# An attention stage reordered on TensorE, with small moves on ScalarE and VectorE around it

## The reference

```
h = rms_norm(x, norm_mix_pre)
z, xbc, dt_raw, q, k, v = jnp.split(h @ w_in, split_at, axis=-1)
s = jnp.einsum('bhcqd,bhckd->bhcqk', qb, k) * scale
s = jnp.where(causal, s, -jnp.inf)
p = jax.nn.softmax(s, axis=-1)
attn = p[:, :, 0] - lam * p[:, :, 1]
o = jnp.einsum('bhqk,bhkv->bhqv', attn, v)
k_mem = (mem_h @ wk)
```

## Time and profile before

| | us |
|---|---|
| median of 3 runs (lowest, highest) | 1418.82 (1418.66, 1419.02) |
| the profiled execution | 1418.83 |
| its span, first to last instruction | 1417.1 |
| TensorE busy | 1399.2 |
| VectorE busy | 943.2 |
| ScalarE busy | 666.8 |

### The profile page before, as it was taken

How to read it: one execution, slowest core, us unless ns; L and a number is a source line. 1 busy time by engine, 2 the same in 40 slices (tenths; PEclk the granted TensorE clock), 3 DMA queues, 4 the chain that set the end, 5 groups by cost and what they waited for, 6 DMA issues and landing times.

```text
span 1417.1 us, 19418 instructions
## 1 busy us (share of the span) xinstructions
PE 1399.2 (99%) x7146; PEld 1172.0 (83%) x7146; DVE 943.2 (67%) x1516; ACT 666.8 (47%) x1297; POOL 70.6 (5%) x122
## 2 busy tenths in 40 slices
PE   9999999999989999999999999999999999999997
PEld 7889888876779888888888888888888888888886
DVE  4785577748878336344555888886665685467897
ACT  6225332347776325333433765454444654444443
POOL 0000000010002002010001200000000000000011
PEclk9999999999999999999999999999999999999999
DMA  9212333320014522121133235654443897676463
GB/s 328 67 43 67 91 97 97 97 72 18 1 31 149 208 75 105 60 74 46 60 119 109 100 97 201 218 198 156 164 156 117 297 356 247 225 236 196 153 229 128
DMA packets 98909, 194.45 MB, mean 137 GB/s; under 512 B 11200, under 2 KB 29696, under 8 KB 96768
## 3 DMA queue, kind: packets, MB, share of 16 engines
q1 hardware_dynamic: 87312, 153.30, 32.0%
q10 hardware_dynamic: 11504, 39.92, 8.6%
HBM read 147.01 MB, written 41.98 MB: 133 GB/s over the span
## 4 chain that ended last, share of the span: by engine, by line
PE 91%; DVE 3%; issue 2%; ACT 2%; DMA 1%; SPq 1%; POOL 0%; POOLq 0%; DVEq 0%; ACTq 0%
PE ps L2289 27%; PE ps L2291 27%; PE ps L2290 27%; PE ps L2489 2%; PE ps L2525 1%; PE ps L2355 1%; PE ps L2431 1%; PE ps L2505 1%; DVE nmax L1766 1%; DMA x_in<-in_x_dram 1%; PE ps L2434 1%; ACT junk L858 0%; PE ps L2647 0%; SPq L613 0%; PE ps L2439 0%
## 5 line engine op out<-in xcount | busy, mean ns | idle before, releaser
L2289 PE MATMUL ps<-d_ring 128*128 128x512 f32 x448 | 174.3, 389 | 0.0
L2290 PE MATMUL ps<-d_ring 128*128 128x512 f32 x448 | 174.3, 389 | 0.0
L2291 PE MATMUL ps<-d_ring 128*128 128x512 f32 x448 | 174.3, 389 | 0.0
L2289 PE MATMUL ps<-wh,oph 128*128 128x512 f32 (+1 forms) x448 | 162.5, 363 | 0.0
L2291 PE MATMUL ps<-wh,opl 128*128 128x512 f32 (+1 forms) x448 | 161.0, 359 | 0.0
L2290 PE MATMUL ps<-wl,oph 128*128 128x512 f32 (+1 forms) x448 | 160.4, 358 | 0.0
L2289 PE MATMUL ps<-oph,wh 128*128 128x512 f32 x384 | 152.1, 396 | 1.3 <-DVE opl L1497 1.3
L2291 PE MATMUL ps<-oph,wl 128*128 128x512 f32 x384 | 149.6, 390 | 0.0
L2290 PE MATMUL ps<-opl,wh 128*128 128x512 f32 x384 | 149.5, 389 | 0.0
L1384 ACT ACTIVATE d_ring<-left_raw 128x512 fp32r<-128x512 f32 x112 | 70.2, 627 | 93.7 <-PE ps L2291 74.7
L2137 DVE TENSOR_TENSOR d_ring<-left_raw,d_ring 128x512 fp32r<-128x512 f32 x112 | 78.2, 698 | 52.5 <-ACT d_ring L1384 52.3
(11 more groups left out here) (349 smaller groups left out, 2900.0 us busy)
## 6 DMA issues: line engine op xcount, KB each, us to landing
right_raw<-in_w_down_dram SPq DMA_DIRECT2D x128, 256.0 KB, 4.0
u_kept_s<-us SPq DMA_DIRECT2D x64, 256.0 KB, 3.5
left_raw<-u_kept_s SPq DMA_DIRECT2D x64, 256.0 KB, 2.9
w_blk<-in_w_up_blocks_dram ACTq DMA_DIRECT2D x14, 1024.0 KB, 5.9
left_raw<-u_kept_a SPq DMA_DIRECT2D x48, 256.0 KB, 3.3
raw<-in_w_in_dram SPq DMA_DIRECT2D x16, 512.0 KB, 4.0
u_kept_a<-u SPq DMA_DIRECT2D x24, 256.0 KB, 2.5
x_in<-in_x_dram SPq DMA_DIRECT2D x8, 512.0 KB, 8.7
```

What stands on the lines that cost most here:

```text
L2289: te.matmul(o, lh, rh, start=first, stop=False, skip_group_check=more)
L2290: te.matmul(o, lh, rl, start=False, stop=False, skip_group_check=more)
L2291: return te.matmul(o, ll, rh, start=False, stop=last, skip_group_check=more)
```

## The change

- **Opening, ScalarE.** From the second eighth on, `in_hi(k, 1)` comes before `in_square(k)`; before, the square came first.
- **Attention, TensorE.** In each iteration the value product of step n - 3 comes after the scores and ahead of both transposes of step n - 2. Before, part 0 was ahead of it and part 1 behind it.
- **Filling.** `mk` step 1 moves to the front of iteration 32, into bank 4 (it waits for the exponentials of step 30 only), and is copied to a spare tile by ScalarE within the attention. `mk` step 2 moves into iteration 33, ahead of the last value product. What waits for the last copies is now the first `mix_tile`.
- **ScalarE and VectorE.** The halves of the second weight unit of `mk` are prepared at the start of iteration 32 rather than behind it, the copy of `mk` step 0 comes behind the second exponential, and the first `y_norm` comes one iteration later.

```diff
--- before.py
+++ after.py
@@ -330,7 +330,7 @@
         h_mem = at("h_mem", "TMP", 8192, [P, 2, D])
         kmt = at("kmt", "V", 0, [P, KD, MEM])
         vmt = at("vmt", "V", 8192, [P, KD, MEM])
-        kmt_first = at("kmt_first", "TMP", 13312, [P, MEM])
+        kmt_first = at("kmt_first", "TMP", 13312, [P, 2, MEM])
 
         kmh = at("kmh", "GA", 0, [P, KD, MEM], F32R)
         kml = at("kml", "V", 0, [P, KD, MEM], F32R)
@@ -897,9 +897,11 @@
             first_hi(1, 2)
             for k in range(5, KD):
                 in_hi(k, 0)
-            for k in range(KD):
+            in_square(0)
+            in_hi(0, 1)
+            for k in range(1, KD):
+                in_hi(k, 1)
                 in_square(k)
-                in_hi(k, 1)
 
             for b in range(2):
                 act.wait_ge(rb_done, b + 1)
@@ -1101,9 +1103,18 @@
                     act.wait_ge(sq_done, SQ[("y", NT - 1)] + 1)
                 s.activation(o_part[m % 2][:], mix[:, 4:8, i * P:(i + 1) * P], ACT.Square).then_inc(o_sq, 1)
 
+            def first_keys(st, src):
+
+                act.wait_ge(pj_done, STEP0["mk"] + st + 1)
+                s.activation(kmt_first[:, st, :], src, ACT.Copy).then_inc(ev["mk"], 1)
+
             for n in range(NS + 3):
+                if n == NS:
+                    split_hi(2 * UNIT0["mk"] + 3)
                 if n >= 2 and n - 2 < NS:
                     probs_evac(n - 2, 0)
+                if n == NS:
+                    first_keys(1, ps[:, 4, 0:MEM])
                 if n in (NS, NS + 1):
                     o_square(n - NS)
                 if n >= 3:
@@ -1119,32 +1130,26 @@
                     split_hi(2 * UNIT0["mk"] + 2)
                 if n < NS:
                     attn_exp(n, 0)
-                if n == 1:
-                    act.wait_ge(pj_done, STEP0["mk"] + 1)
-                    s.activation(kmt_first[:], ps[:, 7, MEM:2 * MEM], ACT.Copy).then_inc(ev["mk"], 1)
                 if n < NS:
                     attn_exp(n, 1)
+                if n == 1:
+                    first_keys(0, ps[:, 7, MEM:2 * MEM])
                 if n < 2:
                     y_square(6 + n)
                 if n == 1:
                     act.dma_start(gain_a[:], rows(t["norm_mix_post"][0:1, :])).then_inc(gain_a_loaded, 16)
-                if n == NS:
-                    split_hi(2 * UNIT0["mk"] + 3)
 
 
             act.wait_ge(gain_c_loaded, 16)
-            for n in range(16):
+            act.wait_ge(ev["mk"], 2)
+            after(s.activation(kmt[:, 0:2, :], kmt_first[:], ACT.Copy))
+            for n in range(2, 16):
                 name, st = STEPS[STEP0["mk"] + n]
                 g = STEP0["mk"] + n
                 if n in O_SQUARE_AT:
                     o_square(O_SQUARE_AT[n])
-                if n >= 2:
-                    for q in split_at(name, st):
-                        split_hi(q)
-                if n == 0:
-                    act.wait_ge(ev["mk"], 1)
-                    after(s.activation(kmt[:, 0, :], kmt_first[:], ACT.Copy))
-                    continue
+                for q in split_at(name, st):
+                    split_hi(q)
                 act.wait_ge(pj_done, g + 1)
                 dst = kmt[:, st, :] if name == "mk" else vmt[:, st, :]
                 s.activation(dst, ps[:, bank(g), 0:UC], ACT.Copy).then_inc(ev[name], 1)
@@ -1798,19 +1803,20 @@
             for n in range(NS + 3):
                 if n < NS:
                     attn_max(n, 0)
+                if n == NS:
+                    split_lo(2 * UNIT0["mk"] + 2)
                 if 2 <= n <= NS:
                     attn_comb(n - 1)
                 if n < NS:
                     attn_max(n, 1)
                 if n == 1:
                     attn_comb(0)
-                if n in (0, 2, 3):
-                    y_norm(5 + (n + 1) // 2)
+                if 1 <= n < 4:
+                    y_norm(4 + n)
                 if 1 <= n < 3:
                     y_mean(5 + n)
                 if n == NS:
-                    for half in range(2):
-                        split_lo(2 * UNIT0["mk"] + 2 + half)
+                    split_lo(2 * UNIT0["mk"] + 3)
                 if n == NS + 1:
                     o_mean(0)
             o_mean(1)
@@ -2512,8 +2518,10 @@
                     feature_step("mk", 0, memh, meml, 0, 0, MEM, place=ps[:, 7, MEM:2 * MEM])
                 if n < NS:
                     scores(n)
-                if 2 <= n < NS + 2:
-                    probs_transpose(n - 2, 0)
+                if n == NS:
+                    for c in range(2):
+                        pe.wait_ge(ex_done[c], NS - 1)
+                    feature_step("mk", 1, memh, meml, 1, 0, MEM, place=ps[:, 4, 0:MEM])
                 if n >= 3:
                     k = n - 3
                     i, h = steps[k]
@@ -2525,23 +2533,27 @@
                         ins = te.matmul(o, probs_t[:, k % 2, b, :], vt[:, b, h * P:(h + 1) * P],
                                         start=b == 0, stop=b == i)
                     ins.then_inc(pv_done, 1)
+                if 2 <= n < NS + 2:
+                    probs_transpose(n - 2, 0)
                 if 2 <= n < NS + 2 and steps[n - 2][0] >= 4:
                     probs_transpose(n - 2, 1)
-                if n == NS:
+                if n == NS + 1:
                     for c in range(2):
                         pe.wait_ge(ex_done[c], NS)
-                    feature_step("mk", 1, memh, meml, 1, 0, MEM)
-
-            pe.wait_ge(pt_ev, len(PT_PARTS))
-            pe.wait_ge(o_ev, NS // 2)
+                    feature_step("mk", 2, memh, meml, 0, 0, MEM)
 
             def mix_tile(m):
                 i = MIX_TILES[m]
+                if m == 0:
+                    pe.wait_ge(ev["mk"], 2)
+                    pe.wait_ge(pt_ev, len(PT_PARTS))
+                    pe.wait_ge(o_ev, NS // 2)
                 transpose_tile(TR_MIX + m, lambda k: mix[:, k, i * P:(i + 1) * P])
 
             for n in range(2, 16):
                 name, st = STEPS[STEP0["mk"] + n]
-                feature_step(name, st, memh, meml, st % 2, 0, MEM)
+                if n > 2:
+                    feature_step(name, st, memh, meml, st % 2, 0, MEM)
                 if n in MIX_AT:
                     mix_tile(MIX_AT[n])
```

## The result

The changed kernel took **1426.99 us** (median of 4 runs, 1425.2 to 1427.19), against 1418.92 us (1418.66 to 1419.32) for the kernel before on the same chip: ratio 1.0054, 95% interval 1.0041 to 1.0067. It is slower by 8.1 us. The profiled execution took 1426.89 us, its span is 1425.2 us, 8.1 more than the span before.

A forecast was written before the change was run, and what follows sets the result against it. The prediction took TensorE, busy 99% of the span, as the bound. Opening -1.65, value product +5.4, steps with i = 5 and 4 +0.9 and end +0.5 made 5.1: 1418.8 + 5.1 = 1423.9 us, range 1421.7 to 1426.2.

The forecast's parts named there:

- The value product ahead of both transposes: Attention, eight bank 6 steps: the 1.38 between transposes stays and the product is paid ahead of it, +5.4 us.
- Steps with i = 5 and 4: Attention, part 1 in bank 7: part 0's copy is asked for later, partly covered by a 0.27 gap, +0.9 us.
- rival 1: Later waits are covered, in the i = 5 and 4 loop and at `mk` step 4: 1422.1 us, chance 12%.
- The opening: Start of the kernel: both TensorE stalls on low parts of x go, -1.65 us.
- without its first stall of 0.58 it would be there at about 34.1 itself: Opening: TensorE, freed of its first stall, reaches the point of the second at about 34.1, where operands allow 34.15.
- The end: End of the attention: same instructions, stalls removed and two new waits, +0.5 us in sum.
- The first new stall: End of the attention: value product of step 30, right behind its own transpose, waits for the `o_ev` copy, 1.7 us.
- the removed 2.3: End of the attention: stalls of 0.80 and 1.04 covered by `mk` steps 1 and 2, with smaller savings, -2.3 us.
- The second new one: Behind the attention: TensorE waits before `mk` step 4 for weights from ScalarE's late loop, about 1.1 us.
- 2.4 more until TensorE may use it: Weights of `mk` step 4: 2.4 us from the start of `split_hi` until TensorE may use them.
- rival 2: End of the attention: ScalarE's loop stays late for more than one weight unit, about 1425.5 to 1426.5 us, chance 10%.
- Rival 4: Attention: TensorE's idle moments drop its clock from 2.4 to 1.2 GHz, 1.3 per pair, about 1434 us, chance 2%.

The follow-up runs named there:

- experiment 1: Kernel before, with only the value product moved ahead of both transposes in every iteration: 1425.65 us, ratio 1.0048.
- experiment 2: Changed kernel with the first transpose back ahead of the value product, opening and end still changed: 1418.94 us, ratio 0.9997.
- experiment 6: Changed kernel with the value product back between the transposes only in the eight iterations whose part 1 uses bank 6: 1419.62 us, ratio 1.0003.
- experiment 3: Kernel before, with only the opening changed (copy ahead of the square from the second eighth on): 1417.93 us, ratio 0.9993.
- experiment 4: Changed kernel with the second half of the weights for `mk` steps 4 and 5 prepared one turn earlier on ScalarE and VectorE: 1424.49 us, ratio 1.0038.
- experiment 5: Changed kernel with the edits of experiment 2 and experiment 4 together: 1416.57 us, ratio 0.9982.
- experiment 7: Changed kernel with the edit of experiment 4 in VectorE's loop only: 1426.11 us, ratio 1.0049.

## Why the prediction was right and wrong

The direction, the main mechanism and the rows that would show it were right; the time was 3.1 too low, and outside the range. Point by point:

- **The value product ahead of both transposes: right in kind, 5.4 forecast, 6.1 found.** Up to the scores of iteration 19 the attention took 71.37 instead of 65.23. The distance of the two transposes is the copy's, 1.38 with and without a product in it (experiments 1, 2 and 6), and eight waits of 0.78 stand there. Two sizes were off, by 0.4 each. One is the length of a product: I took 0.89 and 0.67 from differences of the earlier trace rows; moved, it occupies 0.95 and 0.72 from its start to the transpose. The other was put at nothing: the even iterations from 4 to 18 take 0.05 more each, 0.37 together (iteration 6, from scores to scores, is 335.85 to 339.40 for 335.55 to 339.05). The help of 0.4 at the combination in iteration 2 came as forecast (a wait of 1.06 for 1.45), and the distances that were over 1.38 before, as the 1.67 of iteration 3, gave 0.5. The sum closes: 4 x 0.95 + 4 x 0.72 + 0.37 - 0.39 - 0.5 = 6.2, for the 6.1 found.
- **Steps with i = 5 and 4: 0.9 forecast, 0.2 found.** The scores of iterations 19, 21, 23 and 25 start at 384.41, 390.01, 395.62 and 401.23, 5.6 apart as before (379.19, 384.80, 390.40, 396.00); the 0.17 comes in iterations 25 and 26, behind which the scores are at 406.34 (before at 400.94). The gap of 0.27 was read rightly, and it is used up. What was mis-sized is the delay that it has to take in. ScalarE in the changed kernel, iteration 21:

```profile
387.16 0.87 ACT L1093 ACTIVATE probs_t<-ps 128x512 f32<-128x512 f32 x2 [0.56 <-PE ps L2511]
...
388.88 0.90 ACT L1078 ACTIVATE probs<-ps,nmax 128x768 f32<-128x768 f32 x1
```

  The copy of part 0 starts 2.75 behind the scores for 2.26 before, 0.49 later; but the transposes of both parts now stand in a row, so the two copies follow each other at once, and the next exponential starts 0.76 behind the first of them (387.92) instead of 0.94 (387.06 to 388.00 before). Only 0.31 comes through, about what the gap holds: the second exponential starts 4.47 behind the scores, for 4.46. The half of rival 1 on this loop came nearly true, for another reason than its own. This miss and the one above cancel, 6.3 forecast for the two and 6.31 found, and that is luck.
- **The opening: -1.65 forecast, -0.9 in this profile, about -1.05 in the median of experiment 3.** The reasoning on ScalarE's slots held, and both stalls went. The step that failed is "without its first stall of 0.58 it would be there at about 34.1 itself": it takes the first product to start at the same time in every run. That start depends on the warming transposes, which took 6.03 to 7.12 us over nine profiles (and in experiment 4 on the product's own low part, 0.27 late). Before, the stalls swallowed the difference: in experiment 1 the first product was 1.08 later than before, and the spread of `rms` came at 42.16 for 42.05. Now it passes through: in the changed kernel and experiments 2, 3, 4, 5 and 6 the first product starts at 7.70 to 8.35 and the spread comes 32.75 to 32.82 behind it, with 7.71 at 40.46 (experiment 3), with 8.35 at 41.10. An earlier start than these gains nothing: with 7.54 the spread is at 40.57 (experiment 7). So about 1.6 is the most that the opening gave in any profile, and the forecast took this best case.
- **The end: +0.5 forecast, +1.3 found, and 1.5 more for the clock.** The first new stall was 1.52 (forecast 1.7), the one that should stay was 0.63 (0.52 before), and the removed 2.3 went. The second new one was 1.99 where I forecast 1.1. The sum closes: -2.3 + 1.52 + 1.99 + 0.11 = 1.3. The step that failed is "2.4 more until TensorE may use it": it was 3.75 (432.79 to 436.54). I worked out ScalarE's queue and got it right: from its last copy of `mix` to the `split_hi` it is 3.64 against 3.7. Behind it I took VectorE's `split_lo` to follow at once, as in the earlier trace rows. ScalarE's and VectorE's queues in the changed kernel:

```profile
429.15 0.38 ACT L1125 ACTIVATE mix<-ps 128x256 f32<-128x256 f32 x1 [2.82 <-PE ps L2533]
...
432.79 1.07 ACT L853 ACTIVATE wh<-raw 128x1024 fp32r<-128x1024 f32 x1
```

```profile
432.99 0.68 DVE L1792 TENSOR_REDUCE stat<-o_part 128x4 f32<-128x512 f32 x1
...
433.98 1.28 DVE L1484 TENSOR_TENSOR opl<-ps,oph 128x512 fp32r<-128x512 f32 x2
435.18 1.22 DVE L1471 TENSOR_TENSOR wl<-raw,wh 128x1024 fp32r<-128x1024 f32 x1
```

  The high part is there at 433.86, its low part starts at 435.18: the sums and the low parts of the first mixed tile stand ahead of it. That is 1.3 more; TensorE's own way was 5.4 long (429.15 to 434.55) instead of 5.0, which takes 0.4 off: 1.1 + 1.3 - 0.4 = 2.0. (A reading beside this sum was wrong and did not enter it: 422.36 to 429.83 is its last three terms and one more step, not all four.) Experiment 7 moved that one instruction and the stall fell by 1.28; rival 2, the wait at the end growing to several units of weights, described what then appeared in experiments 4 and 7.
- **The clock: nothing in the sum, 1.5 found.** Rival 4 had the price per pair of steps and the wrong place; the forecast of the end did not ask what the clock does behind its two stalls. Through the attention with its eight stalls the granted clock read 1.00 in every profile, as the row on the idlest stretch had suggested. In the changed kernel it fell once, behind stalls of 1.52, 0.63 and 1.99, the first of which ends 12.4 us before the last. Experiments 4 and 7, in which the last of these is 0 and 0.71, have no low clock, and experiment 6, with all three stalls, has none either: the stall of 1.99 is what goes with it, but it does not decide it alone. That the clock explains the two groups of experiment 2, and the changed kernel's one run at 1425.2 beside three at 1426.9 to 1427.2, is inferred: from sizes (1.7 and 1.9, for 1.50 in the profiles), and from the mean granted clock of whole runs (0.999 for the run at 1425.2, 0.997 and 0.998 for the three). Only one profile of each kernel was taken. The Trainium skill, "TensorE: Matmul & The Clock Gate", section "A second HAM failure mode: psum-queue depth-cycling", has the clock swinging between its levels in a kernel where the engine is often idle for moments between groups of matmuls. The attention has a pattern of this kind, and no run here shows a swing in it.

Together: 1418.8 - 0.9 + 6.3 + 1.3 + 1.5 = 1427.0, where the forecast had 1423.9. Of the miss of 3.1, 1.5 are the clock, 0.8 the end and 0.75 the opening. The range was too narrow since it held neither a late start of a run nor a low clock at the end.

## What to carry to other kernels

Work that stands in the shadow of a fixed latency is free where it stands, and costs its full length where it is moved; so before moving it, find what the gap that it fills is made of. Here a gap of 1.38 that did not change with the length of the work in it said so in advance.

When a stall is forecast from a producer's queue, follow every engine on the way, the last one above all, and compare its order with what is urgent. A late unit in a loop that is itself late is only passed on when one step is repaired; and where a removed stall had swallowed differences ahead of it, the time now depends on how each run begins.

## What was not expected of the hardware

- A stall of 1.99 us on TensorE, after two of 1.52 and 0.63 in the changed kernel and after the one of 0.63 alone in experiment 2, was followed by some 3 us at a granted clock of 0.50, and cost 1.50 us. In experiment 6 the same stall of 1.99, behind the same 9.80 us of work in 12.42, cost nothing more. What decides between them stays open.
- The 40 warming transposes, with nothing to wait for among them, took 6.03, 6.04, 6.15, 6.33, 6.39, 6.76, 6.81, 6.96 and 7.12 us in nine profiles. Their weight loads read 138 to 232 ns, and the median is 141 where they took 6.03 and 226 where they took 6.96:

```profile
L2363 PEld LDWEIGHTS ps<-ident x40: 139/141/229, 1.6 to 7.3; 128*128 128x128 f32 x40
```

```profile
L2369 PEld LDWEIGHTS ps<-ident x40: 139/226/229, 1.6 to 8.2; 128*128 128x128 f32 x40
```

  (the kernel before, then the changed one; shortest, median and longest ns). The slow ones come first: the stretches of one us from 4 to 7 hold 7, 7 and 8 matmuls in the changed kernel and 9, 12 and 12 in the kernel before. So what differs between runs is how many are slow. That the two lengths are the two levels of the clock would fit, but it is not shown: the granted clock of that stretch reads 1.00 in both. The Trainium skill, "TensorE: Matmul & The Clock Gate", section "What's actually happening", says that the number of matmuls at the low clock at a start differs between runs of one kernel; the spread of 6.03 to 7.12 us agrees with that.
